# Expert stage of a decoder layer: row turns in banks 7 and 5, copies awaited where they are read, and the down product's second block by 64- and 32-row forms

## The reference

```python
def expert_block(args):
    tok, e = args
    gu = t[tok] @ w_gate_up[e] + b_gate_up[e]
    gate = jnp.minimum(gu[:, 0::2], SWIGLU_LIMIT)
    up = jnp.clip(gu[:, 1::2], -SWIGLU_LIMIT, SWIGLU_LIMIT)
    act = (up + 1.0) * gate * jax.nn.sigmoid(SWIGLU_ALPHA * gate)
    return act @ w_down[e] + b_down[e]
```

## Time and profile before

| | |
|---|---|
| median of three runs | 3191.83 us |
| the profiled execution | 3192.96 us |
| its span | 3190.9 us |
| mean granted TensorE clock | 0.935 |
| PE busy | 2776.5 us (87%) |
| DVE, ACT busy | 1158.9, 593.1 us |
| mean DMA rate | 184 GB/s |

### The profile page before, as it was taken

How to read it: one execution, slowest core, us unless ns; L and a number is a source line. 1 busy time by engine, 2 the same in 40 slices (tenths; PEclk the granted TensorE clock), 3 DMA queues, 4 the chain that set the end, 5 groups by cost and what they waited for, 6 DMA issues and landing times.

```text
span 3190.9 us, 41664 instructions
## 1 busy us (share of the span) xinstructions
PE 2776.5 (87%) x12040; PEld 1389.1 (44%) x12041; DVE 1158.9 (36%) x2949; ACT 593.1 (19%) x1582; POOL 182.0 (6%) x188
## 2 busy tenths in 40 slices
PE   6998599999789964999999899999999999999991
PEld 3554466666455631344444334333343443343340
DVE  2776267766446631222221222222212122222125
ACT  1222155555323310010000000100000010000010
POOL 0000000000001010100000100000101000000100
PEclk9999599999899956999999999999999999999995
DMA  8222553030201007766555966677876766646746
GB/s 300 69 65 72 124 156 89 16 75 15 94 34 40 34 14 291 272 230 250 193 188 185 339 241 227 226 291 270 324 272 255 264 222 226 251 172 228 294 182 270
DMA packets 295909, 586.97 MB, mean 184 GB/s; under 512 B 79006, under 2 KB 117918, under 8 KB 274312
## 3 DMA queue, kind: packets, MB, share of 16 engines
q1 hardware_dynamic: 255805, 542.87, 48.1%
q0 software_dynamic: 21152, 38.50, 3.6%
q10 hardware_dynamic: 18859, 4.42, 0.6%
HBM read 559.44 MB, written 69.88 MB: 197 GB/s over the span
## 4 chain that ended last, share of the span: by engine, by line
PE 51%; issue 3%; DMA 3%; DVE 3%; ACT 1%; ACTq 0%; DVEq 0%; POOL 0%; POOLq 0%; SPq 0%
PE ps L1820 30%; PE ps L1904 17%; PE ps L1916 2%; PE ps L1793 2%; DVE x L1778 1%; DMA d_ys<-ys_e,dst 1%; DVE gu L1715 1%; DMA xg<-d_h,src 1%; ACT aT L1629 1%; PE ps L1798 1%; DMA wg<-in_w_gate_up 1%; ACT xT_e L1609 0%; DVE gg L1718 0%; DVEq L1509 0%; DMA src<-d_tok 0%
## 5 line engine op out<-in xcount | busy, mean ns | idle before, releaser
L1820 PE MATMUL ps<-wg,xT_e 128*64 128x512 f32 (+2 forms) x4032 | 1034.3, 598 | 33.8 <-issue 30.4
L1820 PEld LDWEIGHTS ps<-wg,xT_e 128*64 128x64 f32 (+2 forms) x4032 | 398.6, 147 | 639.3 <-issue 634.6
L1904 PE MATMUL ps<-w_rows,aT 128*128 128x512 f32 x1152 | 527.9, 614 | 40.9 <-issue 23.9
L1715 DVE TENSOR_TENSOR gu<-ps,bias 64x512 f32<-64x512 f32 (+2 forms) x252 | 173.6, 689 | 654.8 <-PE ps L1820 632.6
L1904 PEld LDWEIGHTS ps<-w_rows,aT 128*128 128x128 f32 x1152 | 220.4, 196 | 309.6 <-issue 285.6
L1651 ACT ACTIVATE ss<-gg 128x256 f32<-128x256 f32 x146 | 60.8, 416 | 1289.5 <-DVE gg L1718 747.8
L1759 DVE COPY ys_e<-ps 128x1024 f32<-128x1024 f32 x36 | 44.1, 1225 | 622.3 <-PE ps L1904 622.3
L442 PE MATMUL ps<-w_in,hT_a 128*128 128x430 f32 x512 | 194.6, 533 | 6.3 <-DVE hT_a L345 6.3
L793 PE MATMUL ps<-ident_t,sc 128*128 128x128 f32 x880 | 152.1, 290 | 28.2 <-ACT sc L859 24.7
L859 ACT ACTIVATE sc<-sc,nm 128x640 f32<-128x640 f32 (+15 forms) x256 | 161.5, 633 | 53.1 <-DVE nm L901 53.1
L1793 PE MATMUL ps<-ident_e,xg 128*128 128x128 f32 x392 | 72.4, 323 | 101.5 <-DMA xg<-d_h,src 48.4
(11 more groups left out here) (293 smaller groups left out, 2489.3 us busy)
## 6 DMA issues: line engine op xcount, KB each, us to landing
wg<-in_w_gate_up SPq DMA_DIRECT2D x128, 2048.0 KB, 8.1
w_rows<-in_w_down SPq DMA_DIRECT2D x128, 1024.0 KB, 7.9
bias<-in_b_gate_up SPq DMA_DIRECT2D x32, 1024.0 KB, 9.7
wg<-d_ys SPq DMA_DIRECT2D x8, 2048.0 KB, 12.4
d_bias<-d_rev SPq DMA_DIRECT2D x1, 10368.0 KB, 37.9
w_in<-in_w_in SPq DMA_DIRECT2D x1, 6880.0 KB, 23.9
x_a<-in_x POOLq DMA_DIRECT2D x8, 512.0 KB, 3.7
kn<-d_kn SPq DMA_DIRECT2D x8, 512.0 KB
```

The source lines that it names most:

```text
L1715: read = dve.tensor_tensor(gu[part, :], ps[part, BANK[k][j], :], bias[part, cols], ALU.add)
L1820: mm = pe.matmul(ps[g * kind:(g + 1) * kind, BANK[k][j], :], xT[:, kk, t0:t0 + kind], wg[:, j * groups + g, kk, :], start=(kk == 0), stop= ...
L1904: mm = pe.matmul(ps[:, 2 + 2 * b + h, :], aT[:, j, b * P:(b + 1) * P], wd[:, c, j % 2, h * 512:(h + 1) * 512], start=(j == 0), stop=(j == ...
```

## The change

The row turns go to banks 7 and 5. TensorE's waits on f's copies leave the place ahead of the row turns: one goes to the turn of f's third activation, the others to the product that reads them. The down product is made by segment, in the order f, h, g, q: f by the 128-row form into banks 2 and 3, h by the 64-row form into bank 4, g by the 64-row form into bank 5, q by a 32-row form into bank 5, four matmuls of 256 columns side by side. The late turns are made at chunk 1, f's copy is awaited at chunk 3 and h's at chunk 2. `s_down` becomes four semaphores; the eviction goes by segment.

```diff
-        s_down = [sem(f"e_down{b}") for b in range(2)]
+        s_down = {k: sem(f"e_down_{k}") for k in "fhgq"}
...
+        ROW_BANK = (7, 5)
+        ARMS = {64: "h", 96: "hq", 128: "f", 160: "fq", 192: "fh", 224: "fhq", 256: "fhg"}
...
-                            for b in range(2):
-                                sp.wait_ge(s_down[b], CREDIT + NCH * i + c + 1 - NCH)
+                            for k in "fhgq":
+                                sp.wait_ge(s_down[k], CREDIT + NCH * i + c + 1 - NCH)
                                 hold(sp, e.sp_passed)
...
+                        def take(k, i, last):
+                            dve.wait_ge(s_down[k], CREDIT + NCH * i + NCH)
+                            if k == "f":
+                                done = dve.tensor_copy(ys[:, 0, :].rearrange("p (c n) -> p c n", c=2), ps[:, 2:4, :])
                             else:
+                                second, row, parts, bank = int("f" in last), {"h": 0, "g": P // 2, "q": P // 2 if "h" in last else 0}[k], 4 if k == "q" else 2, 4 if k == "h" else 5
+                                r, w = P // parts, D // parts
+                                for g in range(parts):
+                                    done = dve.tensor_copy(ys[row:row + r, second, g * w:(g + 1) * w], ps[g * r:(g + 1) * r, bank, 0:w])
+                            if k == last[-1]:
+                                done.then_inc(s_y, 2)
...
-                        if k == 1 and busy is not None:
-                            pe.wait_ge(s_aTc["f"], busy)
...
-                                        pe.wait_ge(s_aTc["f"], CREDIT + 4 * i + 1)
+                                        pe.wait_ge(s_aTc["f"], CREDIT + 4 * i + 2)
...
-                        pe.wait_ge(s_aTc["f"], CREDIT + 4 * i + 2)
-                        hold(pe, e.pe_passed)
...
-                        pe.wait_ge(s_aTc["f"], CREDIT + 4 * i + 3)
-                        hold(pe, e.pe_passed)
-                        for k, have in (("q", 1), ("g", 2), ("h", 1)):
-                            pe.wait_ge(s_aTc[k], CREDIT + SEG[k][2] * i + have)
-                            hold(pe, e.pe_passed)
+                        def copied(k, n):
+                            pe.wait_ge(s_aTc[k], CREDIT + SEG[k][2] * i + n)
+                        def rows_copied(k):
+                            pe.wait_ge(s_xTc, CREDIT + 4 * i + 4 + k)
                         def last_turn(k, j):
                             pe.wait_ge(s_a[k], CREDIT + SEG[k][2] * i + SEG[k][2])
-                            pe.wait_ge(s_xTc, CREDIT + 4 * i + 4 + 3)
+                            rows_copied(3)
                             turn_act(k, j)
-                            pe.wait_ge(s_aTc[k], CREDIT + SEG[k][2] * i + SEG[k][2])
...
+                        def whole():
+                            copied("f", 3)
                             for c in range(NCH):
                                 pe.wait_ge(s_wd[c], CREDIT + 16 * i + 16)
+                                if c == 1:
+                                    last_turn("f", 3)
+                                if c == 3:
+                                    copied("f", 4)
...
+                                mm.then_inc(s_down["f"], 1)
+                        def part(k, parts, bank, t0):
+                            r, w = P // parts, D // parts
+                            if k == "h":
+                                copied("h", 1)
+                            else:
+                                rows_copied(4)
+                                copied(k, SEG[k][2])
                             for c in range(NCH):
                                 pe.wait_ge(s_wd[c], CREDIT + 16 * i + 16)
+                                if c == 1 and k == "h":
+                                    last_turn("h", 1)
+                                if c == 2 and k == "h":
+                                    copied("h", 2)
                                 for j in (2 * c, 2 * c + 1):
+                                    for g in range(parts):
+                                        mm = pe.matmul(ps[g * r:(g + 1) * r, bank, 0:w], aT[:, j, t0:t0 + r], wd[:, c, j % 2, g * w:(g + 1) * w],
                                                        start=(j == 0), stop=(j == JD - 1))
+                                mm.then_inc(s_down[k], 1)
...
                         with pe.If(hash_ > 0):
+                            part("h", 2, 4, 128)
...
+                        with pe.If(hasg > 0):
+                            part("g", 2, 5, 192)
...
+                        with pe.If(hasq > 0):
+                            part("q", 4, 5, 192)
+                        with pe.Else():
+                            pe.sem_inc(s_down["q"], NCH)
```

More of the change, by code:

```diff
@@ L1505, in stage_experts @@
         ACT_BANK = {"q": (2,), "g": (2, 4), "h": (3, 7), "f": (6, 7, 6, 7)}
-        ARMS = {64: "h", 96: "qh", 128: "f", 160: "qf", 192: "hf", 224: "qhf", 256: "ghf"}
+        ROW_BANK = (7, 5)
+        ARMS = {64: "h", 96: "hq", 128: "f", 160: "fq", 192: "fh", 224: "fhq", 256: "fhg"}
         def rows_left(eng, i):
@@ L1608, in copy_rows @@
                         for at, to, w in moves:
-                            cp = act.activation(xT[:, 2 * k:2 * k + 2, to:to + w], ps[:, 7 - k % 2, :].rearrange("p (k n) -> p k n", k=2)[:, :, at:at + w], ACT.Copy)
+                            cp = act.activation(xT[:, 2 * k:2 * k + 2, to:to + w], ps[:, ROW_BANK[k % 2], :].rearrange("p (k n) -> p k n", k=2)[:, :, at:at + w], ACT.Copy)
                         cp.then_inc(s_xTc, 1)
@@ L1752, in _ @@
                             none("f")
[L1754 to L1757, removed]
-                            else:
-                                done = dve.tensor_copy(ys[:, b, :].rearrange("p (c n) -> p c n", c=2), ps[:, bank:bank + 2, :])
-                            done.then_inc(s_y, add)
+                        def take(k, i, last):
+                            dve.wait_ge(s_down[k], CREDIT + NCH * i + NCH)
+                            if k == "f":
+                                done = dve.tensor_copy(ys[:, 0, :].rearrange("p (c n) -> p c n", c=2), ps[:, 2:4, :])
+                            else:
+                                second, row, parts, bank = int("f" in last), {"h": 0, "g": P // 2, "q": P // 2 if "h" in last else 0}[k], 4 if k == "q" else 2, 4 if k == "h" else 5
[4 more added lines that the diff above has]
+                                done.then_inc(s_y, 2)
                         def evict(rows):
                             dve.wait_ge(s_sd, CREDIT + i)
[L1764 to L1770, removed]
+                            for k in ARMS[rows]:
+                                take(k, i, ARMS[rows])
                         by_rows(dve, n, evict)
@@ L1783, in _, with turn_rows @@
             def _(pe):
-                def turn_rows(i, nb, busy=None):
+                def turn_rows(i, nb):
                     pe.wait_ge(s_x, 32 * i + 32)
@@ L1792, in turn_rows @@
                                 c = 2 * k + kk
-                                mm = pe.transpose(ps[:, 7 - k % 2, kk * PASS + b * P:kk * PASS + (b + 1) * P], xg[:, b, c * P:(c + 1) * P], ident[:, :])
+                                mm = pe.transpose(ps[:, ROW_BANK[k % 2], kk * PASS + b * P:kk * PASS + (b + 1) * P], xg[:, b, c * P:(c + 1) * P], ident[:, :])
                         mm.then_inc(s_xT, 1)
@@ L1878, in _ @@
                             turn_act("h", 0)
-                        pe.wait_ge(s_aTc["f"], CREDIT + 4 * i + 2)
-                        hold(pe, e.pe_passed)
                         with pe.If(after > P):
-                            turn_rows(i + 1, 2, CREDIT + 4 * i + 3)
+                            turn_rows(i + 1, 2)
                         with pe.Else():
-                            turn_rows(i + 1, 1, CREDIT + 4 * i + 3)
-                        pe.wait_ge(s_aTc["f"], CREDIT + 4 * i + 3)
@@ L1886, in _ @@
[L1886 to L1889 removed]
+                            turn_rows(i + 1, 1)
+                        def copied(k, n):
+                            pe.wait_ge(s_aTc[k], CREDIT + SEG[k][2] * i + n)
+                        def rows_copied(k):
+                            pe.wait_ge(s_xTc, CREDIT + 4 * i + 4 + k)
@@ L1891, in last_turn @@
                         def last_turn(k, j):
                             pe.wait_ge(s_a[k], CREDIT + SEG[k][2] * i + SEG[k][2])
-                            pe.wait_ge(s_xTc, CREDIT + 4 * i + 4 + 3)
+                            rows_copied(3)
                             turn_act(k, j)
-                            pe.wait_ge(s_aTc[k], CREDIT + SEG[k][2] * i + SEG[k][2])
-                        def whole(b, turn):
+                        def whole():
+                            copied("f", 3)
@@ L1898, in whole @@
                             for c in range(NCH):
                                 pe.wait_ge(s_wd[c], CREDIT + 16 * i + 16)
-                                if c == 2:
```

(38 more changed lines are left out.)

## The result

The changed kernel takes 3175.45 us, the median of six runs (3172.11 to 3177.6), against 3190.60 for the kernel before in the same comparison: a ratio of 0.9947, 95% interval 0.9936 to 0.9959, 13 to 20 us less where 28 were forecast. A second comparison later gave 0.9934 (0.9921 to 0.9948), 17 to 25 us less. The profiled execution took 3172.11 us, 20.8 less than that of before; its stages ahead of the experts, whose code is the same, ran 3.6 us longer (the first row turns start at 1229.78 for 1226.22).

A forecast was written before the change was run, and what follows sets the result against it. TensorE matmuls were taken as half of the chain, gate-up and down products leading. Gains 12.6 + 13.9 + 27 + 68 less 69, 21 and 3.5 gave 28 us: 3164 from 3192, range 3112 to 3192.

The forecast's parts named there:

- Term 1: Down product's late turns: f's and h's copies awaited where read, not right behind the turn; gains 12.6 and 13.9 us.
- Term 2: Row turns before the down product: banks 7 and 5 and a shorter tail gain 27 us; waits behind ScalarE's order stay.
- Term 3: Down product by segment forms: q takes 3.5 us at 0.054 us a matmul; gains 68 us.
- Term 4: Loop turn after short forms: too little queued work covers the sequencer's 5.3 us way round; costs 69 us.
- Term 5: Gate-up after the new gaps: TensorE's clock falls each time, 1.4 us for each of 15 gaps; costs 21 us.
- the longer queue: Rival at the loop turn: sequencer hands over the whole q form early, gap only 1.85 us; 3113 us, chance 0.15.
- the dear q form: Rival in the down product: 256-wide q matmuls no cheaper than 512-wide, part takes 7 us; 3215 us, chance 0.10.
- the dearer gap: Rival at the loop turn: slow clock lasts twice as long, way round longer; 28 us more, 3192 us, chance 0.13.
- the six qh passes before q: Gate-up loads as second bound: in these passes 1.2 to 3 us can be won, not more.

The follow-up runs named there:

- e7: Changed kernel with the copies of f's and h's late turns awaited right behind the turn again: 3198.57 us, 1.0017 of the kernel before.
- e1: Changed kernel with the down product's forms of before, but waits, late turns and row banks as changed: 3145.51 us, 0.984 of the kernel before.
- e8: Changed kernel with rows turned in banks 7 and 6 and the wait for f's third copy back before the second row group: 3162.71 us, 0.9904.
- e4: Changed kernel with the down product's order turned: q or g first, then h, f last: 3096.23 us, 0.9704 of the kernel before.
- e10: e4 with the semaphore for an absent f raised before the h units, so gate-up loads start earlier: 3082.24 us, 0.9657 of the kernel before.
- e3: Changed kernel with q made by the 64-row form, computing 32 rows nobody reads: 3152.89 us, 0.9874 of the kernel before.

## Why the prediction was right
The direction, the likeliest mechanism and the range held; the forecast gain of 28 us was too large by 7 to 13, for 15 to 21 were measured.

*Term 1* (26.5 us): e7 gives it back as 22 to 27 us. Right.

*Term 2* (27 us): near in its sum, and right in naming ScalarE's order as what stays. By the timeline a qhf pass needs 3.38 us from its last turns to the product (1374.82 to 1378.20) where it took 4.30, 0.92 and not 0.75; the qh pass 5.25 for 6.79, 1.54 and not 1.1. In 20 passes of the one kind and nine of the other these would be 32 us, where 25 were forecast. Terms 1 and 2 together were 53.5 less 1.5 for pass 1, and e1 measured 49: in e1 TensorE waits some 6 us longer than before for weights, gathered rows and aa (22.9 for 16.6), so that the sum came out so near is in part luck. And the step "two groups go ahead, ScalarE's copies start some 0.5 us sooner" put part of this down to the bank. e8 shows as short a stretch without it, and is 10 to 14 us faster: the bank was forecast to help a little and cost that much.

*Term 3* (68 us): 71 by the groups. 64 matmuls in 3.66 us, the last one's tail included, are the 0.054 us apiece that the earlier trace rows let one expect. The 62 ns per matmul that the Trainium skill names for the case that hardware decode is off (TensorE: Matmul & The Clock Gate, section on 56 ns against 53.3) do not bind here.

*Term 4* (69 us): gaps of 3.83 to 3.88 us before q for 4.05, 5.14 to 5.16 before h for 5.3, 5.58 to 5.61 before f for 5.8. Idle time before gate-up grew by 79 us; against that the stalls of 8.7 us for gathered rows and 4.5 for aa went, as forecast. Right.

*Term 5* (21 us): this is the term that was mis-sized. "Part of the slow stretch lies in the gap, so I take 1.4 of the 1.7" failed. The unchanged gate-up product was 36.3 us longer busy. Behind the 19 parts for q with a gap, the units took 38 us over the full rate, 2.0 on the mean: most 1.4 to 1.9 us (22.65 against 20.96 for 128 matmuls), eight 2.4 to 2.9 (37.79 against 34.89 for 160), one nothing. So after the longer gaps the slow stretch was often longer than after the 2.69 us of before, not shorter. With 2 a gap and the 15 gaps I counted the forecast would have been 19 us, with the 36 us that were measured 13. Nor does a gap of this length make the clock fall each time, as I had it: here are nearly equal gaps ahead of a first f unit, before and after, and the one gap of the changed kernel that cost nothing.

```profile
1800.27 13.99 PE L1820 MATMUL ps<-wg,xT_e 128*128 128x512 f32 x32 [3.47 <-issue]
```

```profile
1804.62 15.69 PE L1818 MATMUL ps<-wg,xT_e 128*128 128x512 f32 x32 [3.45 <-issue]
...
2906.53 20.96 PE L1818 MATMUL ps<-wg,xT_e 128*32 128x512 f32 x128 [3.83 <-issue]
```

What decides it beside the gap's length, no run here shows.

Of the rivals, the longer queue is out (the gaps are there), the dear q form is out, and the dearer gap was half true: the way round was as long as forecast, the clock was dearer. That the six qh passes before q stand near their loads was right too: three of their gaps of 3.8 us end with a landing, in e4 seven waits do, and e10 shortens them.

## What to carry to other kernels
A saving on an engine that works off a queue is worth its time only if the sequencer (the part of the engine that takes branches and hands instructions to the queue) still gets round the loop in the time that the queued work lasts: look up the last instruction handed over, the branch behind it and the first instruction of the next turn, and compare that way with queued instructions times their duration. Put the short forms first and the long ones last ahead of a loop turn; here that order turned a change worth 0.5 to 0.7% into one worth 3%. A gap that appears can cost more than its own length, in the slow clock behind it: 2 us on the mean here.

## What the runs showed of the hardware
More useless work was faster: q at twice the rows saved some 20 us (e3). TensorE's sequencer could be ahead by about 20 float32 matmuls of the trace, whatever they last: 20 at 0.107 us in the earlier trace rows. In the changed kernel the branch behind a q part runs at 2038.6 and the last matmul of the part starts at 2039.7, 1.1 us or 20 at 0.054 (of the part's 64 matmuls the second line counts those from 2037 us on):

```profile
L1938 PEldq COMPARE_BRANCH  x1: 169/169/169, 2038.6 to 2038.6; - x1
...
L1922 PE MATMUL ps<-w_rows,aT x57: 379/379/379, 2036.6 to 2039.7; 128*32 128x256 f32 x57
```

Behind an h part these are 2397.9 and 2401.7, 3.8 us or 18 at 0.21. The Trainium skill (TensorE: Matmul & The Clock Gate, queue depths) names 64 entries; counted as loads and matmuls together these traces show some 40, so the lead was shorter than that number lets one expect. Reading three registers from the plan once more cost 2.0 us a turn where nothing covered it (3.86 to 5.82). And moving a transpose to a free bank bought nothing (e8): the waits before the row turns only changed their name, 53.1 us before and 62.5 in the changed kernel, while ScalarE, which copies the rows out, kept its own order.
